# Hybrid DeltaNet layer: the masked decay inputs earlier on Pool, the output norm in eight chunks on two engines

## The reference

```python
gc = jnp.cumsum(to_chunks(g), axis=-1)
diff = gc[..., :, None] - gc[..., None, :]
decay = jnp.where(incl, jnp.exp(jnp.where(incl, diff, 0.0)), 0.0)
kk = jnp.einsum('nbhid,nbhjd->nbhij', kc, kc)
a_mat = jnp.where(strict, bc[..., :, None] * kk * decay, 0.0)
sol = lax.linalg.triangular_solve(a_mat, rhs, left_side=True, lower=True, unit_diagonal=True)
...
y = rms_norm(o, w) * jax.nn.silu(gate)      # gated_head_norm, per head and token
```

## Time and profile before

| what | us |
|---|---|
| median of 3 runs (range) | 2733.16 (2729.6 to 2743.19) |
| the profiled execution, whole | 2735.79 |
| its span in the profile | 2734.0 |
| PE busy | 2547.3 (93%) |
| DVE busy | 1404.5 (51%) |
| POOL busy | 866.0 (32%) |
| ACT busy | 808.6 (30%) |

### The profile page before, as it was taken

The page is one execution under the profiler, slowest core; times in us unless marked ns, Lnnn a source line. Parts: engine busy times, 40 slices in busy tenths (PEclk is TensorE's granted clock), DMA queues, the critical chain, the costliest instruction groups (busy, mean ns, idle before and its releaser), DMA issues. The chain is left out here.

```text
span 2734.0 us, 40299 instructions
## 1 busy us (share of the span) xinstructions
PE 2547.3 (93%) x16246; PEld 2120.3 (78%) x16246; DVE 1404.5 (51%) x2110; ACT 808.6 (30%) x1745; POOL 866.0 (32%) x580
## 2 busy tenths in 40 slices
PE   6999999999898989898989898999999999998999
PEld 4768887888687868686868787787778888886887
DVE  5783664114355555554646464335775555555242
ACT  4223553101254444445444444311121111112010
POOL 1443652332313132323222222234633333331121
PEclk9999999997899999999999999999999999999999
DMA  7222232231000000000000000232431111112443
GB/s 266 72 67 86 109 116 77 70 107 40 9 17 32 9 32 9 32 9 32 9 32 25 16 24 17 88 105 93 139 119 47 55 47 47 48 48 87 126 134 94
DMA packets 52646, 177.01 MB, mean 65 GB/s; under 512 B 5360, under 2 KB 14960, under 8 KB 51184
## 3 DMA queue, kind: packets, MB, share of 16 engines
q1 hardware_dynamic: 50160, 170.24, 19.3%
q10 hardware_dynamic: 2304, 4.20, 0.4%
HBM read 148.20 MB, written 20.97 MB: 62 GB/s over the span
## 5 line engine op out<-in xcount | busy, mean ns | idle before, releaser
L201 PE MATMUL late_ps<-h_hi,late_w_hi 128*128 128x512 f32 x784 | 305.6, 390 | 5.9 <-ACTq L127 3.2
L203 PE MATMUL late_ps<-h_hi,late_w_lo 128*128 128x512 f32 x784 | 305.0, 389 | 0.0
L202 PE MATMUL late_ps<-h_lo,late_w_hi 128*128 128x512 f32 x784 | 305.0, 389 | 0.0
L1403 PE MATMUL late_ps<-h_hi,dn_w_hi 128*128 128x512 f32 (+1 forms) x640 | 252.5, 394 | 5.6 <-issue 5.6
L1403 PE MATMUL late_ps<-h_lo,dn_w_hi 128*128 128x512 f32 (+1 forms) x640 | 254.9, 398 | 0.0
L1403 PE MATMUL late_ps<-h_hi,dn_w_lo 128*128 128x512 f32 (+1 forms) x640 | 253.1, 395 | 0.0
L184 POOL CAST late_w_hi<-late_w_raw 128x1024 fp32r<-128x1024 f32 x76 | 79.4, 1045 | 501.7 <-issue 376.0
L191 POOL TENSOR_TENSOR late_w_lo<-late_w_raw,late_w_hi 128x1024 fp32r<-128x1024 f32 x76 | 204.0, 2684 | 6.1
L2444 DVE SCALAR_TENSOR_TENSOR ffn_u<-ffn_pad,vectors,ffn_u 128x1024 f32<-128x1024 f32 x88 | 194.5, 2210 | 3.1
L201 PEld LDWEIGHTS late_ps<-h_hi,late_w_hi 128*128 128x128 f32 x784 | 147.2, 188 | 37.4 <-issue 6.7
L202 PEld LDWEIGHTS late_ps<-h_lo,late_w_hi 128*128 128x128 f32 x784 | 147.2, 188 | 30.7 <-issue 0.2
(11 more groups left out here) (360 smaller groups left out, 6117.5 us busy)
## 6 DMA issues: line engine op xcount, KB each, us to landing
late_w_raw<-in_w_up SPq DMA_DIRECT2D x44, 512.0 KB, 3.5
down_w_raw<-in_w_down SPq DMA_DIRECT2D x32, 704.0 KB, 4.4
late_w_ada<-in_w_ada SPq DMA_DIRECT2D x8, 2048.0 KB, 8.3
dn_w_raw<-in_w_dn SPq DMA_DIRECT2D x32, 512.0 KB, 3.8
w_ada<-in_w_ada SPq DMA_DIRECT2D x8, 1024.0 KB, 11.1
at_w_raw<-in_w_mg_at SPq DMA_DIRECT2D x16, 512.0 KB, 4.0
late_w_raw<-in_w_mg_dn SPq DMA_DIRECT2D x16, 512.0 KB, 3.7
late_w_raw<-in_w_out SPq DMA_DIRECT2D x16, 512.0 KB, 3.8
```

Of the source, the lines that this page charges most:

```text
L201: pe.matmul(out, self.hi[j][:, k, :], xh, start=(k == 0), stop=False)
L202: pe.matmul(out, self.hi[j][:, k, :], xl, start=False, stop=False)
L203: mm = pe.matmul(out, self.lo[j][:, k, :], xh, start=False, stop=(k == self.kt - 1))
L1403: mm = pe.matmul(bank[at_bank(s)][:, 0:n], wt[:, k, :], x[:, k, t0:t0 + n], start=(rest == 0), stop=(rest == GROUP_MM - 1))
```

## The change

In POOL's list `masked_g` 2 and 3 stand ahead of `units`, directly behind masks 0 and 1, and mask 4 follows the first select. The output norm is made by eight instructions of 128 columns, each with the reciprocals of its chunk as a per-partition scalar: chunks 0 to 3 by `tensor_scalar` on DVE, chunks 4 to 7 by `activation` with `Copy` and `scale` on ACT, which stand between ACT's root and `act_tail` and wait for the reciprocal (`orec`). PE waits for DVE's four ahead of its first four turns and for ACT's four (`ona`) ahead of the other four, and DVE waits for `ona` before it overwrites `o_acc`. PE's list is otherwise as it was. Semaphores, buffers and arithmetic of everything else stay.

```diff
-        xev, yac, osq, gts = C("x_copied"), C("y_copied"), C("o_std"), C("gate_silu")
+        xev, yac, osq, gts, ona = C("x_copied"), C("y_copied"), C("o_std"), C("gate_silu"), C("o_normed_by_act")
...
             vd.wait(pe, h * 20 + 20)
-            onr.wait(pe, h + 1)
             for b in range(2):
+                (onr, ona)[b].wait(pe, h + 1)
                 for n in range(4):
                     mm = pe.transpose(bank[b][:, n * P:(n + 1) * P], o_norm[:, 4 * b + n, :], mats[:, C_ID, :])
                 mm.then_inc(otd.sem, 1)
...
             act.activation(o_stat[:, 2, :], o_stat[:, 1, :], ACT.Sqrt).then_inc(osq.sem, 1)
+            orec.wait(act, h + 1)
+            for c in range(XCH // 2, XCH):
+                ins = act.activation(o_norm[:, c, :], o_acc[:, c, :], ACT.Copy, scale=o_stat[:, 0, c:c + 1])
+            ins.then_inc(ona.sem, 1)
             if fill:
                 act_tail(act, h + 1)
...
             orec.wait(dve, h + 1)
-            dve.tensor_tensor(o_norm[:, :, :], o_acc[:, :, :], o_stat[:, 0, :].unsqueeze(2).broadcast_to([P, XCH, P]),
-                              ALU.mult).then_inc(onr.sem, 1)
-            onr.wait(dve, h + 1)
+            for c in range(XCH // 2):
+                ins = dve.tensor_scalar(o_norm[:, c, :], o_acc[:, c, :], o_stat[:, 0, c:c + 1], None, ALU.mult)
+            ins.then_inc(onr.sem, 1)
+            ona.wait(dve, h + 1)
...
-            for bt in range(2):
+            for bt in range(4):
                 masked_g(bt)
             units()
             for bt in range(BT):
                 bqd.wait(pool, h * 5 + bt + 1)
                 pool.sem_inc(turns, 1)
                 pool.affine_select(flat(bf, bt), flat(bf, bt), pattern=[[0, 4], [1, P]], compare_op=ALU.not_equal,
                                    fill=E_SCALE, base=0, channel_multiplier=-1).then_inc(bfd.sem, 1)
-                if bt + 2 < BT:
-                    masked_g(bt + 2)
+                if bt == 0:
+                    masked_g(4)
```

More of the change, by code:

```diff
@@ L1836, in scalar @@
         def scalar(act):
-            for c in (evac, sil, sqd, stdc, tka, dct, bhd, xev, yac, ed, vd, osq, gts):
+            for c in (evac, sil, sqd, stdc, tka, dct, bhd, xev, yac, ed, vd, osq, gts, ona):
                 c.open(act)
```

## The result

The changed kernel takes 2635.6 us (median of 4 runs, 2631.6 to 2639.4) against 2733.2: a ratio of 0.964 with a 95% interval of 0.961 to 0.967, 98 us less. The forecast was 2614 us in a range of 2600 to 2640. The kernels of this study ran on several chips, on which the kernel before took 2733.2 to 2739.5 us in the median, so differences of a few us between medians are read from the traces.

A forecast was written before the change was run, and what follows sets the result against it. PE's waits for POOL's mask, with half clock behind them, were taken to bound the preparations. Cutting these from 241.55 to 122.5 us takes 119 off the profiled 2735.8, giving 2616.8; the median 2.6 below gives 2614, range 2600 to 2640.

The forecast's parts named there:

- The masks' wait goes: Preparation: PE's three waits a head for POOL's mask, about 3.2 us each, vanish, and the half clock behind them.
- The preparations: Eight heads: 14.8 us in the first, 15.9 in heads two to seven, 12.3 in the last; 122.5 against 241.55.
- ACT's delay: Heads two to seven: four norm copies shift ACT's list by 1.5 us, and PE loses 1.0 us a head.
- The norm on DVE is worth nothing: Head's entrance: the norm product is hidden in seven heads; four chunks on DVE end at 971.3, hidden by 2 us.
- The clock: Preparation and inverse at full clock; dips in the chains could give 3 us less to 9 more over eight heads.
- ACT's whole shift: Upper bound of PE's loss to ACT's copies: 1.5 us a head instead of 1.0, 3 us more in all.
- One wait left: Rival, preparation: one of three waits stays in each head, on mask 4 or an exponential; about 2655 us, chance 0.09.
- half clock in the preparation: Rival: half clock stays despite the waits going, because matmuls are short; up to 7 us a head, 2670, chance 0.06.
- slower than before: Rival, preparation: a late first select makes all three decay products wait for ACT; about 2764 us, chance 0.02.

The follow-up runs named there:

- The one-mask kernel: Against the kernel before, only mask 2 moved ahead of the unit copies, masks 3 and 4 behind the first and second selects, norm as before: 2616.3 us.
- the kernels with extra matmuls: Masks moved, norm as before, each head's first filling matmul repeated with two or four extra copies whose results are overwritten: 2627.0 us with two, 2621.1 with four.
- spread sums: Masks moved, norm as before, the chain's one-column matmuls that sum squares placed between filling matmuls instead of in a row: 2611.6 us.
- the kernel with the masks alone: Against the kernel before, only the change's edits on POOL, the norm left as one 1024-column product on DVE: 2614.4 us.

## Why the prediction was right, and what it mis-sized

- **The masks' wait goes.** Right: no wait for a mask is left, masks 2 and 3 stand ready before they are asked for, and the clock in the preparation is 1.00. First head 14.8 forecast, 14.83 measured. The one-mask kernel adds what the prediction did not see: two of the three waits were consequences of the first.
- **The preparations.** 122.5 us forecast, 124.84 measured: 15.9 against 16.24 in heads two to seven, 12.3 against 12.57 in the last.
- **ACT's delay.** The shift of 1.5 us and the 1.24 for four copies were measured at 1.55 and 1.28. What PE loses by it was put at 1.0 us; it is 1.3, because the filling matmul is held for 0.7 and not 0.6 and the decay product for 0.6 and not 0.4.
- **The norm on DVE is worth nothing.** Right for the change, with a gap in the reasoning: with the unit copies beside it the same code would have held PE for 1.3 us. The forecast used a row of DVE without asking what POOL does at the same moment in the new order; it was the masks that moved POOL away.
- **The clock.** This is the term that was mis-sized. The prediction took the inverse at 1.00 throughout ("With no stall the clock has no reason in these rows to fall") and left the chains' dips at the two of the kernel before. Measured: 9.5 us more in the inverses and 8.2 in the chains. The chains lie inside the 3 less to 9 more that the text gave; the inverses were nowhere in it, though the trace of before had a sign, the last head's inverse at 0.94:

```profile
1658.70:1687.01 28.31, 24.46 (x489) 20.78 (x489) 17.10 (x33) 23.06 (x60) 12.98 (x11) 0.94 0.14 40
```

Forecast for the profiled execution 2616.8, measured 2635.2: 18.4 us, of which 17.7 are these, 2.3 the preparations, and -1.7 the earlier start of the heads. That the time still lies in the range is partly luck: the upper bound of 2640 kept room for ACT's whole shift and for scatter, and the inverses used up that room.
- **The rivals.** One wait left, half clock in the preparation, slower than before: none happened. The second put low clock in the wrong stage: it did come, behind the preparation and not in it.

The second half of the change, forecast to cost 6 to 7 us, costs 21 in this kernel: 8 to 10 directly and 11 to 13 through the clock. The change has 7 and 5 low inverses in its two profiles, and three kernels with masks moved and ACT's part left out have 1 each; but the kernels with extra matmuls or spread sums have 3 to 5 without ACT's part, so how 1.3 us a head brings the low stretches on stays open. The forecast time was hit by the kernel with the masks alone (2614.4), which is a coincidence: its preparations are 6 us shorter than forecast, having no ACT delay, and its chains 5 us longer, five of them being low.

## What to carry to other kernels

When an engine waits again and again at one line for a small instruction of another engine, look at what stands ahead of that instruction in its own list and doesn't feed it: one step of lead can break a loop in which each wait makes the next. Before handing half of a hidden product to an idle engine, ask what is queued behind it there; ACT was 31% busy and still the wrong place, since PE's next steps waited on its list. And when PE becomes dense, count what it saves only after reading the granted clock of the stages behind, because thin spots that kept full clock before may lose it now (0 low inverses of seven before, 7 in the change); here, spreading one-column matmuls and moving filling to the inverse's start took those stretches away.

## What the runs showed of the hardware that was not expected

- A low stretch (1.2 GHz, 1.5 to 1.6 us lost each time) came in a stage with PE busy throughout, right behind the row of ten one-column matmuls (2.29 us), in 44 of 56 chains of the profiles with the masks moved and the row in place, and never behind the row of eight (1.84 us); with both rows spread it came in none of 21 chains (three kernels).
- With it gone from one stage it came up in another (chains 5 to 0, inverses 1 to 5, one profile each), so stages can't be priced for it one by one.
- Four `tensor_scalar` of 128 columns on DVE took 4.62 us beside two copies on POOL and 0.87 us without them, a factor of five, where the old 1024-column product of two tensors went only from 1.22 to 2.97.
- The idle time of PE in the profile understated how much later the waiting matmuls started, 0.92 against 1.32 us, since the modelled ends it counts from lie behind the start of the next matmul.
